# Expert order, the place of the row gather, and the fetch of the last norm's rows in a mixture-of-experts decoder step

## The reference, cut to what matters

```python
hg = einsum('td,edf->tef', t, w_gate)
hu = einsum('td,edf->tef', t, w_up)
act = silu(hg) * hu * comb[:, :, None]     # comb: weight of the pair, zero for experts not taken
out = einsum('tef,efd->td', act, w_down)
x = LN2(alpha * x + gate2 * out) * ln2_g + ln2_b
```

## Time and profile before

| | |
|---|---|
| median of three runs | 1650.84 us (1650.09 to 1652.15) |
| the profiled execution | 1649.67 us, its span 1647.8 us |
| PE busy | 1521.8 us (92%) |
| DVE, ACT, POOL busy | 505.2, 245.2, 142.0 us |
| DMA | 559.69 MB, mean 340 GB/s |
| bodies run | 31 |

### The profile page before, as it was taken

How to read it: one execution, slowest core, us unless ns; L and a number is a source line. 1 busy time by engine, 2 the same in 40 slices (tenths; PEclk the granted TensorE clock), 3 DMA queues, 4 the chain that set the end, 5 groups by cost and what they waited for, 6 DMA issues and landing times.

```text
span 1647.8 us, 22763 instructions
## 1 busy us (share of the span) xinstructions
PE 1521.8 (92%) x8533; PEld 656.2 (40%) x8534; DVE 505.2 (31%) x1428; ACT 245.2 (15%) x531; POOL 142.0 (9%) x215
## 2 busy tenths in 40 slices
PE   3899999999999899999999999999999999999974
PEld 2457555456344444433333333333333333333321
DVE  6467345222233265731212121121111211211216
ACT  2220000042213322111111110100100100100111
POOL 6001000131210230010000000000000000000010
PEclk9999999999699899899999999999999999999997
DMA  9995788873186879988996999999999999999943
GB/s 293 386 387 182 282 301 292 291 219 103 55 302 251 317 267 395 397 336 337 422 422 279 423 421 421 421 422 421 421 422 421 421 421 422 422 421 422 422 169 157
DMA packets 119287, 559.69 MB, mean 340 GB/s; under 512 B 15657, under 2 KB 20553, under 8 KB 64921
## 3 DMA queue, kind: packets, MB, share of 16 engines
q1 hardware_dynamic: 100800, 510.20, 77.8%
q0 software_dynamic: 17952, 46.05, 8.2%
q10 hardware_dynamic: 482, 2.70, 0.6%
HBM read 565.78 MB, written 42.37 MB: 369 GB/s over the span
## 4 chain that ended last, share of the span: by engine, by line
PE 60%; DMA 35%; DVE 3%; issue 1%; ACT 1%; POOL 0%; SPq 0%; POOLq 0%; DVEq 0%; ACTq 0%
DMA ring<-in_exp_w_up 31%; PE bank L752 14%; PE bank L2336 6%; PE bank L2244 5%; PE bank L770 5%; PE bank L2093 4%; PE bank L346 3%; PE bank L726 3%; DMA ring<-in_w_in 2%; PE bank L2287 2%; PE bank L2176 2%; DMA ring<-in_ada_w 2%; PE bank L739 1%; PE bank L836 1%; PE bank L2071 1%
## 5 line engine op out<-in xcount | busy, mean ns | idle before, releaser
L752 PE MATMUL bank<-ring,BC 128*64 128x512 f32 x1984 | 455.4, 594 | 36.2 <-DMA ring<-in_exp_w_up 35.2
L752 PEld LDWEIGHTS bank<-ring,BC 128*64 128x64 f32 x1984 | 147.2, 137 | 338.5 <-issue 267.7
L770 PE MATMUL bank<-ring,BC 128*64 128x512 f32 x992 | 219.7, 595 | 0.0
L614 DVE TENSOR_TENSOR BC<-BC,bank 64x512 f32<-64x512 f32 x31 | 21.4, 691 | 463.1 <-ACT BC L692 463.1
L726 PE MATMUL bank<-H,MOD 128*64 128x512 f32 x512 | 131.6, 592 | 0.3 <-DVE H L1950 0.3
L770 PEld LDWEIGHTS bank<-ring,BC 128*64 128x64 f32 x992 | 68.5, 137 | 127.7 <-issue 123.9
L550 POOL DMA_INDIRECT y_dram<-BC,y_row x31 | 29.9, 966 | 857.6 <-DVE y_row L624 741.6
L2336 PE MATMUL bank<-ring,MT 128*128 128x512 f32 x224 | 101.8, 608 | 1.0 <-issue 0.8
L2244 PE MATMUL bank<-ring,MT 128*128 128x512 f32 x192 | 85.4, 598 | 1.0 <-ACT X L1166 1.0
L692 ACT ACTIVATE BC<-bank 64x512 f32<-64x512 f32 x31 | 18.2, 588 | 451.5 <-PE bank L752 451.5
L2093 PE MATMUL bank<-MT,ring 128*128 128x288 f32 x256 | 66.2, 422 | 6.3 <-DMA ring<-in_w_in 4.0
(11 more groups left out here) (543 smaller groups left out, 1459.1 us busy)
## 6 DMA issues: line engine op xcount, KB each, us to landing
ring<-in_exp_w_gate SPq DMA_DIRECT2D x128, 1024.0 KB
ring<-in_exp_w_up SPq DMA_DIRECT2D x128, 1024.0 KB
ring<-in_exp_w_down SPq DMA_DIRECT2D x128, 1024.0 KB
ring<-in_ada_w SPq DMA_DIRECT2D x96, 1024.0 KB
ring<-in_w_in SPq DMA_DIRECT2D x20, 1024.0 KB
y_dram<-con POOLq DMA_DIRECT2D x20, 1024.0 KB, 34.1
ring<-in_w_out SPq DMA_DIRECT2D x16, 1024.0 KB
ring<-in_ssm_glu_w SPq DMA_DIRECT2D x4, 1024.0 KB
```

The costliest lines, as they stand in the source:

```text
L752: mm = pe.matmul(bank[64 * i:64 * i + 64, 2, :], xT[:, q // 2, k % 4, 64 * (q % 2):64 * (q % 2) + 64], ring[:, at, 512 * (k % 4):512 * (k ...
L770: mm = pe.matmul(bank[64 * (c % 2):64 * (c % 2) + 64, 4 + c // 2, :], aT[:, j, :], ring[:, at, 512 * c:512 * c + 512], start=(j == 0), sto ...
```

## The change

1. *Order of the experts.* An expert with two blocks (not expert 0) gets the key 4.5 + 6 w, where w counts such experts from 1; every other expert has its number as key. Blocks and places follow the keys. The new first block and place of an expert are sums over the experts with a smaller key, made on DVE with each expert on its own partition, and spread to all partitions by one matmul with ones (`order_ps`). The slots of the pairs are computed in the order of numbers for the first selection, and moved by 64 times the difference of the first blocks before the second.
2. *The gather in pieces.* In `body(e)` PE waits at the head for `sel_ready` of the next block, and gathers its rows in front of the four pairs of gate and up chunks: two parts ahead of the first pair, one ahead of the second and one ahead of the third, the sample rows ahead of the fourth. The copies `rows_out` move ahead of silu and its product on ACT and DVE. `turn(e + 1)` stands right behind gate and up, ahead of the transposes of the activation.
3. *The last norm's rows.* Their ten DMAs stand behind the six final gathers on POOL. DVE waits for them ahead of L918.

```diff
+WIDE_FROM, WIDE_STEP = 4.5, 6.0
...
-            pool.wait_ge(S("x1_ready"), 2)
-            pool.dma_start(GE[:, 0, :], a["ln2_g"].to_broadcast([P, D])).then_inc(S("ln2_in"), 16)
-            pool.dma_start(GE[:, 1, :], a["ln2_b"].to_broadcast([P, D])).then_inc(S("ln2_in"), 16)
-            for x, t in (("ln2_g", g2_q), ("ln2_b", b2_q)):
-                for q in range(4):
-                    pool.dma_start(t[32 * q:32 * q + 32, :], a[x][:, 512 * q:512 * q + 512].to_broadcast([32, 512]))\
-                        .then_inc(S("ln2_in"), 16)
...
+                rows_out(e + 1)
                 dve.wait_ge(S("sg_ready"), e + 1)
                 V.tensor_tensor(AC[hi, :], SG[hi, :], bank[hi, 2, :], ALU.mult).then_inc(S("act_ready"), 1)
-                rows_out(e + 1)
...
-            at = rc[0:NBLK, R_P:R_P + 1]
-            for i, (upto, part) in enumerate(((end_of, some), (place, ones[:, 0:E]), (place, xe))):
-                dve_chain.tick(V.scalar_tensor_tensor(out=RT[0:NBLK, 4, i, :], in0=upto[0:NBLK, :], scalar=at,
-                                                      in1=part[0:NBLK, :], op0=ALU.is_le, op1=ALU.mult,
-                                                      accum_out=xf[0:NBLK, i:i + 1]))
-            go(V.tensor_scalar(rsm[:, 6, 0, 0:2], slot_f[:, 2, :], 4.0, rc[:, R_Q:R_Q + 1], ALU.mult, ALU.add),
-               V.tensor_scalar(rsm[:, 6, 1:3, 0:2], slot_f[:, 0:2, :], float(SLOTS), None, ALU.add),
-               V.tensor_scalar(behind[0:1, 0:1], end_of[0:1, E - 1:E], float(FULL), None, ALU.subtract),
-               V.tensor_scalar(row_edge[:, 0:E], first_of, 2.0 * SLOTS, float(NO_ROW), ALU.mult, ALU.add),
-               V.tensor_copy(row_at, rc[:, R_W:R_W + 1]),
-               V.memset(edge_sign[:, 0:E], 1.0), V.memset(edge_sign[:, E:], -1.0))
+            some, wide, number = xk[:, :, 0], xk[:, :, 1], rc[:, R_E:R_E + E]
+            key, key_at, to_first, first, end, named = (RT[:, i, j, :] for i, j in
+                                                        ((3, 0), (3, 1), (3, 2), (8, 0), (8, 1), (8, 2)))
+            own, spare = RT[0:E, 5, 0:2, :], RT[0:E, 5, 2, :]
+            go(V.memset(xk[:, 0, 1:2], 0.0))
+            go(V.tensor_tensor_scan(key_at, ones[:, 0:E], wide, 0.0, ALU.mult, ALU.add))
+            go(V.scalar_tensor_tensor(out=key_at, in0=key_at, scalar=WIDE_STEP, in1=number, op0=ALU.mult, op1=ALU.subtract))
+            go(V.scalar_tensor_tensor(out=key_at, in0=key_at, scalar=WIDE_FROM, in1=wide, op0=ALU.add, op1=ALU.mult))
+            go(V.tensor_tensor(key, key_at, number, ALU.add), V.tensor_tensor(named, some, number, ALU.mult))
+            go(V.scalar_tensor_tensor(out=spare, in0=ident[0:E, 0:E], scalar=1.0, in1=key[0:E, :],
+                                      op0=ALU.mult, op1=ALU.mult, accum_out=xf[0:E, 3:4]))
+            go(*[V.scalar_tensor_tensor(out=RT[0:E, 4, i, :], in0=key[0:E, :], scalar=xf[0:E, 3:4], in1=n[0:E, :],
+                                        op0=ALU.is_lt, op1=ALU.mult, accum_out=xf[0:E, 4 + i:5 + i])
+                 for i, n in enumerate((xe, some))])
+            V.tensor_tensor(own, spread_mid(ident[0:E, 0:E], 2), spread(xf[0:E, 4:6], E), ALU.mult)\
+             .then_inc(S("own_ready"), 1)
+            dve.wait_ge(S("order_ps"), 1)
+            go(V.tensor_copy(first, bank[:, 3, ORDER_AT:ORDER_AT + E]))
+            go(V.tensor_tensor(to_first, first, first_of, ALU.subtract), V.tensor_tensor(end, first, xe, ALU.add),
+               V.tensor_scalar(row_edge[:, 0:E], first, 2.0 * SLOTS, float(NO_ROW), ALU.mult, ALU.add))
             go(V.scalar_tensor_tensor(out=row_edge[:, E:], in0=count, scalar=2.0, in1=row_edge[:, 0:E],
                                       op0=ALU.mult, op1=ALU.add))
+            rows_out(0)
+            at, place = rc[0:NBLK, R_P:R_P + 1], bank[0:NBLK, 3, ORDER_AT + E:ORDER_AT + 2 * E]
+            for i, (upto, op, part) in enumerate(((end[0:NBLK, :], ALU.is_le, some), (place, ALU.is_equal, named),
+                                                  (place, ALU.is_lt, xe))):
+                dve_chain.tick(V.scalar_tensor_tensor(out=RT[0:NBLK, 4, i, :], in0=upto, scalar=at, in1=part[0:NBLK, :],
+                                                      op0=op, op1=ALU.mult, accum_out=xf[0:NBLK, i:i + 1]))
+            go(V.tensor_scalar(behind[0:1, 0:1], end_of[0:1, E - 1:E], float(FULL), None, ALU.subtract),
+               V.tensor_reduce(behind[0:1, 1:2].unsqueeze(2), some[0:1, :].unsqueeze(1), AX.X, ALU.add))
             V.nop().then_inc(S("xf_ready"), 1)
-            rows_out(0)
+            turned_out(0)
             dve.wait_ge(S("xf_ps"), since("xf_ps") + 1)
             V.tensor_copy(rint[0:1, I_EXTRA:I_EXTRA + 1], behind[0:1, 0:1]).then_inc(S("rint_ready"), 1)
-            V.tensor_copy(rint[0:1, I_LIVE:I_N], place[0:1, E - 1:E]).then_inc(S("rint_ready"), 1)
+            V.tensor_copy(rint[0:1, I_LIVE:I_N], behind[0:1, 1:2]).then_inc(S("rint_ready"), 1)
             V.tensor_scalar(rint[0:1, I_PLACE:I_FIRST], bank[0:1, 3, 0:2 * NBLK], E - 1.0, None, ALU.min)\
              .then_inc(S("rint_ready"), 1)
             V.tensor_copy(rint[0:1, I_FIRST:I_LIVE], bank[0:1, 3, 2 * NBLK:2 * NBLK + E]).then_inc(S("rint_ready"), 1)
-            turned_out(0)
+            go(V.tensor_tensor(product, both, to_first.unsqueeze(1).unsqueeze(1).to_broadcast([P, 2, 3, E]), ALU.mult))
+            moved = rsm[:, 7, :, 0:2]
+            go(V.tensor_reduce(moved.rearrange("p b i -> p i b").unsqueeze(3), product, AX.X, ALU.add))
+            go(V.scalar_tensor_tensor(out=slot_f[:, :, :], in0=moved, scalar=float(SLOTS), in1=slot_f[:, :, :],
+                                      op0=ALU.mult, op1=ALU.add))
+            go(V.tensor_scalar(rsm[:, 6, 0, 0:2], slot_f[:, 2, :], 4.0, rc[:, R_Q:R_Q + 1], ALU.mult, ALU.add),
+               V.tensor_scalar(rsm[:, 6, 1:3, 0:2], slot_f[:, 0:2, :], float(SLOTS), None, ALU.add),
+               V.tensor_copy(row_at, rc[:, R_W:R_W + 1]),
+               V.memset(edge_sign[:, 0:E], 1.0), V.memset(edge_sign[:, E:], -1.0))
             go(V.tensor_copy(slot_i[:, 0:2, :], rsm[:, 6, 1:3, 0:2]), V.tensor_copy(slot_i[:, 2, :], rsm[:, 6, 0, 0:2]))
             select(1)
...
+                rows_out(e + 1)
                 act.wait_ge(used, len(plan) + e * RING + 8)
                 nc.scalar.activation(SG[hi, :], bank[0:64, 2, :], ACT.Silu).then_inc(S("sg_ready"), 1)
-                rows_out(e + 1)
...
-            def gather(it, finished=False):
+            def gather_first(it):
 
                 pe.wait_ge(S("sel_ready"), it + 1)
-                for i in ((1, 0) if finished else (0, 1)):
-                    if finished:
-                        pe.wait_ge(S("h2_ready"), 8 - 4 * i)
+                for i in (1, 0):
+                    pe.wait_ge(S("h2_ready"), 8 - 4 * i)
                     for b in range(2):
-                        for h in range(2):
-                            q = 2 * i + h
-                            pe.matmul(bank[64 * h:64 * h + 64, i, :], sel[:, b, :], H[:, b, 512 * q:512 * q + 512],
-                                      start=(b == 0), stop=False)
+                        gather_rows(i, b)
+                pe.wait_ge(S("own_ready"), 1)
+                pe.matmul(bank[:, 3, ORDER_AT:ORDER_AT + 2 * E], ones[0:E, :],
+                          RT[0:E, 5, 0:2, :].rearrange("p i e -> p (i e)"), start=True, stop=True)\
+                  .then_inc(S("order_ps"), 1)
+                gather_samples()
+
+            def gather_rows(i, b):
+
+                for h in range(2):
+                    q = 2 * i + h
+                    pe.matmul(bank[64 * h:64 * h + 64, i, :], sel[:, b, :], H[:, b, 512 * q:512 * q + 512],
+                              start=(b == 0), stop=False)
+
+            def gather_samples():
...
+                pe.wait_ge(S("sel_ready"), e + 2)
                 for k in range(KD):
+                    if k == 0:
+                        gather_rows(0, 0)
+                        gather_rows(0, 1)
+                    elif k == 4:
+                        gather_rows(1, 0)
+                    elif k == 8:
+                        gather_rows(1, 1)
+                    elif k == 12:
+                        gather_samples()
...
-                gather(e + 1)
+                turn(e + 1)
                 pe.wait_ge(S("rint_ready"), since("rint_ready") + 4)
                 pe.wait_ge(S("act_ready"), e + 1)
                 for j in range(4):
                     mm = pe.transpose(bank[:, 3, SLOTS * j:SLOTS * j + SLOTS], AC[hi, j:FE:4], ident[hi, 64:128])
                 mm.then_inc(S("at_ps"), 1)
-                turn(e + 1)
...
-            gather(0, True)
+            gather_first(0)
+            turn(0)
             pe.wait_ge(S("xf_ready"), since("xf_ready") + 1)
             for i in range(3):
                 mm = pe.matmul(bank[0:1, 3, NBLK * i:NBLK * i + NBLK], xf[0:NBLK, i:i + 1], ident[0:NBLK, 0:NBLK],
```

(43 more changed lines are left out.)

## The result

The changed kernel takes 1639.93 us (median of four runs, 1638.93 to 1641.29) against 1651.49 us; the ratio is 0.9938, its 95% interval 0.9923 to 0.9953. That is 11.6 us faster, or 10.2 by the ratio. The forecast was 1631.8, its range 1626 to 1642, and 0.60 of the chance stood on 1628 to 1636, which the time misses. The profiled execution spans 1637.1 us, 10.7 less than before.

What follows compares the result with a forecast made beforehand. Bound: TensorE in the first bodies, then the weight stream. Stream -38.1 + 18.0 + 1.7 + 3.65 = -14.75, last body -4.3, tail 0: -19.0, so 1650.84 - 19.0 = 1631.8 us; range 1626 to 1642.

Steps and rivals of the forecast that it cites:

- rival (a): Expert stage: the doubles keep their old stall of 14 us each; +10, 1641.8 us; chance 0.14.
- The bound and the order: Expert stage: early doubles leave the stream dry; with eight and six single experts ahead, both meet TensorE with no lag.
- The catching up: At the start and behind a double: TensorE lags some 17.5 us, wins 3.3 us a body, level after five bodies.
- the prediction's own signs of being wrong: Body without DMA wait over 28 us; dry stretch of 14 us; double meeting a lagging TensorE; L918 waiting for DMA.
- The price of a double: Weight stream at each double: dry 8.2 us, up to 1 us to refill; 9.0 us each, bounds 7 and 14.
- p: Weight stream: the time to load one expert, 30.5 us.
- The last norm's rows: POOL's queue: moved to the tail, 7.4 us come back to the stream; tail cost zero, cover 5 us.
- Rival (b): Tail: the last norm's rows queue behind the gathers and land 2.9 us late; 1634.7 us or more; chance 0.09.
- The body: One run of the expert body on TensorE: 27.2 us after the change, no change, below the stream's 30.5.
- rival (d): Expert stage: a body becomes longer than the stream's 30.5 us an expert; at 31.5, 1660 us; chance 0.06.
- The last body: End of the expert stage: 12.9 us instead of 17.2 behind the last up chunk; gain 4.3 us, once.
- The start: Body 0 waits for the second selection, 3.65 us later, and its first chunk is used another 1.72 us later.

Runs made afterwards that it cites:

- order_off: The changed kernel with no expert marked as wide, so experts are in the order of their numbers again; 1661.94 us, ratio 1.0065.
- adjacent: The changed kernel with keys 10.5 and 10.75, so both doubles stand behind expert 10, one after the other; 1656.71 us, ratio 1.0038.
- step8: The changed kernel with keys 10.5 and 18.5, so seven single bodies instead of six lie between the doubles; 1639.68 us, ratio 0.9943.
- rows_early: The changed kernel with the ten DMAs of the last norm's rows back ahead of the first scatter; 1650.13 us, ratio 0.9993.
- only_rows_late: The kernel before with only the last norm's rows moved behind the final gathers; 1651.82 us, ratio 1.0012.
- keep_busy: The changed kernel with four matmuls into an unread bank between the order lists' transposes and body 0; 1639.28 us, ratio 0.9932.
- wait_later: The changed kernel with the gather's pieces one pair later and PE's wait for the next selection ahead of the second pair only; 1636.17 us, ratio 0.9895.

## Why the prediction was right, step by step

**The number** was right by its range, not by its size: of the 19.0 us forecast about half came (11.6 by the medians, 10.2 by the ratio, 9.5 by R), and 1639.93 lies nearer to rival (a)'s 1641.8 than to 1631.8. The mechanism held; the terms missed mostly one way.

**The bound and the order** were read rightly. That two early doubles held the stream at TensorE's pace is borne out by order_off (1661.94) and adjacent (D2 56.3), and that eight and six single experts ahead of them suffice by step8 (no difference).

**The catching up** was not. The prediction let TensorE win 3.3 us a body and be level after five; at 28.15 us a body it wins 30.46 - 28.15 = 2.3, and needs about seven, as the waits above show. Two of the prediction's own signs of being wrong came with it: a body without a DMA wait took over 28 us, and the second double met a TensorE that had not waited for the stream since the first. That this cost only some 0.5 us is luck in the choice of six, which lies just short of enough; with the five that the sum allows it would have been some 2.3 us more, an estimate from the 2.3 us a body.

**The price of a double** was the largest mis-sized term: 9.0 us forecast, 11.8 and 12.0 measured, 5.8 together. Windows of 1 us around the first (columns as in the earlier trace rows) show it.

```profile
944.00:945.00 1.00, 0.68 (x4) 0.35 (x6) 0.96 (x5) 0.68 (x2) 0.00 (x0) 1.00 0.70 295
945.00:946.00 1.00, 1.00 (x6) 0.30 (x4) 0.76 (x6) 0.00 (x0) 0.00 (x0) 1.00 0.37 156
946.00:947.00 1.00, 1.00 (x8) 0.35 (x6) 0.10 (x1) 0.00 (x0) 0.00 (x0) 1.00 0.18 74
947.00:948.00 1.00, 1.00 (x8) 0.39 (x6) 0.00 (x0) 0.00 (x0) 0.00 (x0) 1.00 0.04 16
...
954.00:955.00 1.00, 1.00 (x6) 0.30 (x4) 0.00 (x0) 0.00 (x0) 0.18 (x1) 1.00 0.27 111
955.00:956.00 1.00, 1.00 (x8) 0.34 (x6) 0.00 (x0) 0.00 (x0) 0.00 (x0) 1.00 1.00 410
956.00:957.00 1.00, 1.00 (x8) 0.41 (x6) 0.00 (x0) 0.00 (x0) 0.00 (x0) 1.00 0.02 4
957.00:958.00 1.00, 1.00 (x6) 0.30 (x4) 0.00 (x0) 0.00 (x0) 0.00 (x0) 1.00 0.27 33
958.00:959.00 1.00, 1.00 (x8) 0.34 (x6) 0.00 (x0) 0.00 (x0) 0.00 (x0) 1.00 0.71 205
959.00:960.00 1.00, 1.00 (x8) 0.41 (x6) 0.00 (x0) 0.00 (x0) 0.00 (x0) 1.00 0.95 401
```
The last data of the old expert trickle in by about 947.5. The next issue is at 956.87, so the stream is dry for 9.4 us, not 8.2; what passes from 954 to 957 is POOL's scatter of a full block (0.52 MB). Then it lacks (0.13 x 422 + 389 + 217 + 21) / 422 = 1.6 us until it is full at 960, not up to 1. The first body of the double ends later than taken (0.45 us, see the last body below), and the refilling I had priced without a row. These make 2.0 of the 2.8 us that each double costs more. The rest is the slow end of the stream, which the prediction took as sharp: it lacks 2.2 us of full rate from 944 to 947.5, and the scatter gives 1.2 back. Counted by bytes the gap closes: from 944 to 956.87 pass 1.07 MB, 2.5 us at the full rate, so 10.3 us are lost there and 1.6 behind the issue, 11.9 against 11.8 measured. The second double's 12.0 are TensorE's eight bodies, and stand for its price only as far as the two are equal (11.5 in step8). p, taken as 30.52 and measured as 30.46 here, shifts 0.5 us between the double and its eight experts. The Trainium skill ("DMA: Bandwidth & Descriptors", Specifications) gives some 0.6 us to the first byte of such a queue; the trace agrees if that is counted from the end of the 0.34 us that the issue takes: windows of 0.2 us have the first data at 957.8 to 958.0 here and at 1182.9 to 1183.1 behind the second double, 0.9 to 1.0 us behind the issue's start, where the prediction took 0.7.

**The last norm's rows** brought 7.9 us where 7.4 were forecast, by rows_early, and nothing in the kernel before, by only_rows_late. Rival (b) did not come: the tail has no wait for them. Their landings in the tail, median us:
```profile
GE<-in_ln_g POOLq DMA_DIRECT2D x1, 1024.0 KB, 12.3
GE<-in_ln_b POOLq DMA_DIRECT2D x1, 1024.0 KB, 13.3
X<-in_ln_g POOLq DMA_DIRECT2D x4, 64.0 KB, 13.1
X<-in_ln_b POOLq DMA_DIRECT2D x4, 64.0 KB, 12.3
ring<-y_dram,slot_i POOLq DMA_INDIRECT x6, 10.1
```
The last is issued by 1603.1 and lands by about 1615; VectorE's first use of them (L918 before, L964 now) comes at 1620.92. The estimate from the table of the Trainium skill ("DMA: Bandwidth & Descriptors", Bandwidth, Measured), 19.9 us for ten transfers one behind another, would have made it 5.2 us late. The trace doesn't agree: the ten are issued in 5.1 us (1597.94 to 1603.07), they land 12 to 13 us after their issue (medians), so they overlap, and 17 us after the first issue all are there, the gathers' data with them. The gathers' own landing went from 7.1 to 10.1 us, but the tail is 52.75 us against 52.3, and 52.0 in only_rows_late, so this costs nothing that can be told.

**The body**: 27.2 us forecast, 28.15 measured. The sample calls take 1.02 us between pairs where I took 0.8, the last pair 3.63 instead of 3.43, and the transposes of the activation 0.68 instead of 0.26, since their end is now waited for. It cost little here: 28.15 is still under 30.46, so rival (d) did not come; what it took away is the margin in catching up, above. **The last body**: the third pair waits until 1565.96, so the last up chunk lands near 1571.0 (TensorE's last wait for one, of its weight loads, ends at 1570.91), and the down product ends at 1584.35, 13.35 us behind; 12.9 forecast, 17.2 before.

**The start**: +5.35 us forecast, +7.6 measured. The selection came when forecast, 7.5 us behind the sample call (7.6 by my sum); the missing 2.3 us are the granted clock, and keep_busy gives back 2.4.

**The sum**: forecast -19.0, measured -10.7 on the span. 5.8 are the doubles, 2.3 the clock, 0.45 the last body, 0.45 the tail. These make 9.0 us; the part ahead of the stage was 1.2 us shorter, which leaves 7.8 of the 8.3 us between forecast and measurement, and 0.5 us unplaced. Neither rival (a), 14 us a double, nor the forecast's 9 holds, but a price between them.

**What stays open**: 1.4 us of rows_early; what the new order is worth by itself on the kernel before, which was not run; and what an earlier first use is worth at a double: 1.7 us was expected, 0.2 to 1.3 us was seen, and D1 scatters by as much.

## What to carry to other kernels

When a buffer holds one unit of a stream, a unit that is used twice costs the stream the whole second pass unless the consumer has caught up; so put such units as many single ones apart as the consumer needs (lag over gain a unit), and no further; and take the gain from the unit's time after the change, as it is a small difference of two large times (0.95 us more on a body of 27.2 took nearly a third of the 3.3 us that each was to win). A transfer that is free in a stretch held by another engine is not free once that engine is out of the way, so price it by its share of the DMA engines and undo it in both kernels. Of an added wait count the idle time and also what the clock takes from the work behind it.

## What I had not expected of the hardware

The granted clock fell to 0.50 behind an idle time of 3.97 us, and four gather calls took 3.68 us; the same calls behind 0.34 us of idle time took 1.94 at 1.00. In wait_later it fell behind an idle time of only 2.10 us, too. After 9.4 us without work the stream came back over 3 us from the issue (4, 33, 205, 401 GB/s in the windows of 1 us from 956 on). At the other two restarts, issued at 701.43 and 1182.10, the windows behind look different (131, 279, 451 from 702 on; 147, 418 from 1183 on), but each loses the same 1.6 us of full rate from its issue.
